# Short convolution's input projection as seven products of halves, with both modulation streams started later

## The chip, the cores and the metric

The kernel runs on one core of a Trainium2 chip. The metric is the device time of one execution in microseconds (us); of several runs the median is taken. TensorE is called PE, VectorE DVE, GpSimd POOL. SyncE (SP) only issues transfers from device memory here.

## The reference

The program is a network in float32 on 512 tokens of width 1024: first four layers with attention mixers, then a second block of two layers. The second block's layer 0 is a hybrid mixer and a feed-forward network; its layer 1 is the short convolution and a feed-forward network. What the change touches is this:

```python
mod = silu(c) @ ada_w[i] + ada_b[i]                  # 1024 -> 6 x 1024, for layer i
sh1, sc1, g1, sh2, sc2, g2 = split(mod, 6)

def shortconv_mixer(h, w_in, conv_w, w_out):         # w_in: 1024 x 3072
    gb, gc, u = split(h @ w_in, 3, axis=-1)
    return (gb * dw_conv(gc * u, conv_w)) @ w_out    # 3 taps over the tokens

x = x + g1 * shortconv_mixer(modulate(rms_norm(x, norm_mix[i]), sh1, sc1), ...)
x = x + g2 * swiglu(modulate(rms_norm(x, norm_ffn[i]), sh2, sc2), ...)
```

## The kernel before

Everything is kept with features on the 128 partitions and tokens along them, so `x` and the normed, modulated `h` are eight tiles of 128x512. Each engine has its own program, and semaphores order them.

**Weights.** SP loads slots of up to 1 MB (1024 input features by 256 output features) into the two halves of `ring`. The load of slot i+1 waits until PE has begun with slot i (`slot_begun`, given by the first matmul on a slot). For the short convolution SP loads twelve slots, for each of four groups g of 256 features the gate gc, then u, then gb.

**The short convolution before.** `short_convolution` on PE runs `pair_of_tiles` for each slot (L1680): two tiles of eight matmuls 128x512 each (L727), in banks 0 and 1 in turn. ScalarE copies the two gate tiles to `sc_gate`; DVE multiplies the tiles of u by them into the padded `sc_pad` (L3161), runs `convolve` (three operations over 512 tokens, all in SBUF, L2856 to L2858) into `sc_sum`, and multiplies the tiles of gb by it into `og` (L3169). `out_projection_of_parts` (L921) then multiplies `og` by the output weights; its first eight products need og's tiles 0 to 3, the next ones wait for tiles 4 to 7 one by one.

**Seven products, in the feed-forward networks.** `ffn` computes a product of a slot (both dimensions halved: a11, a12, a21, a22) and `h` (input features and tokens halved: b11, b12, b21, b22) in seven products of halves instead of eight. A slot is a chunk: seven parts of four matmuls 128x256 (`part`, L1588), in the order p1 = a11 b11, p2 = a12 b21, p6, p5, p7, p3, p4; `first_parts` runs the first two, `other_parts` the other five. The five need sums: four of weights, which DVE makes for each chunk from the slot (`sum_weights`, four operations 128x512, L3024 to L3031, told by `weights_summed`), and four differences of `h` made once (`sum_moving`, L3044, told by `moving_summed`). A chunk has three PSUM banks (`BANK_SETS`), and p6 is accumulated on what p1 left in its bank, and so on; so ScalarE copies three states of banks (`snaps`, L2225, told by `snap_read`), and DVE adds them to the final states: after p2 (L3070), after p7 (L3075) and after p3 (L3077); the fourth quarter is ready after p4. PE waits for the addition after p7 before it runs p4 in the same bank, and for a chunk's weight sums before `other_parts`. In `gated_pair` of the network, DVE's weight sums for the next chunk stand between the addition after p2 and the one after p7. The first two chunks run their first parts one behind the other, while the differences and sums are made.

**Modulation.** POOL computes `mod` in nine jobs (`job`), each a stream of 24 steps of 512 KB: a transfer into one of two buffers (L657), a multiplication by a column of silu(c) (TENSOR_SCALAR, L669), and an addition to `ada_sum` (TENSOR_TENSOR, L673), both with all operands in SBUF. A job begins when the last one's sums are read (`mods_ready`). Job 7 (`ada_w_2[1]`, first half) therefore begins at the start of the first network (`ffn(7)` on PE), and is wanted at its end; job 8 (second half) begins at the start of the short convolution and is wanted at the end of its output projection. Both are wanted in `result_squares`, which sums squares of the result for the norm on PE and turns the modulation sums into columns (L782). Behind it the norm runs: root on ScalarE, reciprocal on DVE (L2406), spread on PE, `normed` on DVE (L2416) and `shift` on ScalarE (L1784), tile by tile, each told by `h_ready`.

## Time and profile before

| | us |
|---|---|
| median of 3 runs | 2848.08 |
| lowest, highest | 2843.29, 2850.89 |
| the profiled execution | 2844.35 |
| its span, first to last instruction | 2842.5 |
| PE busy | 2699.3 (95%) |
| DVE busy | 1314.0 (46%) |
| POOL busy | 1069.4 (38%) |
| ScalarE busy | 659.5 (23%) |

| stretch of the span | from, to (us) |
|---|---|
| first network, its first two chunks | 1753.15 to 1789.90 |
| first network, all | 1753.15 to 2177 |
| short convolution, products of the input projection | 2184.54 to 2349.42 |
| its output projection | 2349.42 to 2404.44 |
| last network, its first two chunks | 2412.33 to 2442.93 |

In the profile, lengths are in us, times are counted from the first instruction, and what stands in brackets behind an instruction is how long its engine idled before it and what released it. A matmul of float32 shows as two records. The mean granted clock of TensorE is 0.980 of full speed.

### The profile page before, as it was taken

The page shows a single profiled execution, that of the slowest core. Times are in us where ns is not written, and L with a number is a line of the kernel's source. Part 1 is how long each engine was busy: PE and PEld are TensorE (multiplying, and loading weights), DVE is VectorE, ACT ScalarE, POOL GpSimd, SP SyncE. Part 2 cuts the span into 40 slices and gives each one's busy share as a digit, 9 for nine tenths or more (in the row PEclk, how much of TensorE's full clock was granted, in tenths as well). Part 3 has the DMA queues.
Part 4 walks back from the last instruction along what each step waited for, and adds up shares of the span by engine and source line. Part 5 has one row for each costly group of instructions (what it writes and reads, how often), then busy time and mean ns, then how long its engine had stood idle before and what let it go on. Part 6 is the DMA issues. An engine that isn't in the chain of part 4 may idle for free.

```text
span 2842.5 us, 32196 instructions
## 1 busy us (share of the span) xinstructions
PE 2699.3 (95%) x11791; PEld 1768.6 (62%) x11791; DVE 1314.0 (46%) x2667; ACT 659.5 (23%) x1575; POOL 1069.4 (38%) x574
## 2 busy tenths in 40 slices
PE   6799999998999999899998899899999999999997
PEld 5356544465666544465645565788887444888886
DVE  7133367334556643333555663443554322433554
ACT  2133123322333432232214522111101001111101
POOL 4785188048583005850683002870001880000000
PEclk7899999999999999999999999999999999999999
DMA  7342343145342114332441003452223542222222
GB/s 244 106 129 92 95 131 115 59 117 147 83 126 53 30 45 124 115 94 59 120 140 38 1 16 99 147 153 89 85 82 99 164 148 74 74 89 85 83 88 71
DMA packets 245112, 277.81 MB, mean 98 GB/s; under 512 B 41427, under 2 KB 217824, under 8 KB 244864
## 3 DMA queue, kind: packets, MB, share of 16 engines
q1 hardware_dynamic: 216000, 175.03, 20.3%
q0 software_dynamic: 28224, 100.86, 11.5%
q8 instruction: 78, 1.28, 0.2%
q14 instruction: 42, 0.34, 0.0%
q10 hardware_dynamic: 768, 0.30, 0.0%
HBM read 274.06 MB, written 2.10 MB: 97 GB/s over the span
## 4 chain that ended last, share of the span: by engine, by line
PE 86%; DVE 4%; DMA 3%; ACT 2%; issue 2%; POOL 1%; SPq 1%; DVEq 0%; ACTq 0%; POOLq 0%
PE psum L1588 27%; PE psum L727 20%; PE psum L921 12%; PE psum L1101 7%; PE psum L895 3%; PE psum L1267 2%; PE psum L782 2%; PE psum L1285 1%; PE psum L907 1%; PE psum L1060 1%; PE psum L1061 1%; PE psum L1419 1%; PE psum L1123 1%; DMA ring<-in_ffn_w_gate 1%; POOL ada_ring L669 1%
## 5 line engine op out<-in xcount | busy, mean ns | idle before, releaser
L657 POOL DMA_DIRECT2D ada_ring<-in_ada_w x192 | 114.8, 598 | 1251.9 <-DVEq L2401 803.6
L727 PE MATMUL psum<-h,ring 128*128 128x512 f32 (+1 forms) x1280 | 538.9, 580 | 16.2 <-DVE arena L2345 4.7
L669 POOL TENSOR_SCALAR ada_ring<-ada_ring,cond 128x1024 f32<-128x1024 f32 x168 | 479.7, 2856 | 8.4 <-POOL ada_sum L673 2.1
L727 PEld LDWEIGHTS psum<-h,ring 128*128 128x128 f32 x1280 | 243.1, 192 | 295.4 <-issue 277.0
L673 POOL TENSOR_TENSOR ada_sum<-ada_sum,ada_ring 128x1024 f32<-128x1024 f32 x168 | 396.9, 2363 | 14.9
L921 PE MATMUL psum<-og,ring 128*128 128x512 f32 x768 | 334.9, 595 | 0.3
L1588 PE MATMUL psum<-og,arena 128*128 128x256 f32 x1152 | 258.6, 379 | 1.7 <-ACT probs L2225 1.7
L921 PEld LDWEIGHTS psum<-og,ring 128*128 128x128 f32 x768 | 145.2, 191 | 180.1 <-issue 180.1
L1588 PEld LDWEIGHTS psum<-og,arena 128*128 128x128 f32 x1152 | 218.7, 190 | 32.1 <-issue 2.4
L1101 PE MATMUL psum<-h,ring 128*128 128x512 f32 x496 | 229.4, 593 | 1.4 <-DVE arena L2473 1.4
L1819 ACT ACTIVATE probsT<-psum 128x128 f32<-128x128 f32 (+3 forms) x232 | 104.5, 451 | 338.9 <-PE psum L895 338.4
L1588 PE MATMUL psum<-h,ring 128*128 128x256 f32 x768 | 178.5, 383 | 1.6 <-DVE mods L2399 0.9
L1588 PEld LDWEIGHTS psum<-h,ring 128*128 128x128 f32 x768 | 146.2, 192 | 26.2 <-ACT h L1784 5.1
L2499 DVE CUSTOM_DVE_ANT_0 psum<-psum,cst 128x128 f32<-128x128 f32 (+1 forms) x192 | 95.3, 498 | 121.3 <-PE psum L1267 83.2
L1101 PEld LDWEIGHTS psum<-h,ring 128*128 128x128 f32 x496 | 87.8, 191 | 81.8 <-issue 81.0
L1852 ACT ACTIVATE sq<-x 128x512 f32<-128x512 f32 x63 | 39.8, 631 | 424.7 <-DVE x L2565 228.4
L2225 ACT ACTIVATE probs<-psum 128x256 f32<-128x256 f32 x132 | 50.8, 385 | 373.5 <-PE psum L1588 373.5
L3101 DVE SCALAR_TENSOR_TENSOR x<-psum,mods,x 128x256 f32<-128x256 f32 x168 | 81.2, 483 | 112.1 <-PE psum L1588 110.8
L2565 DVE SCALAR_TENSOR_TENSOR x<-psum,mods,x 128x512 f32<-128x512 f32 x48 | 36.0, 751 | 204.3 <-PE psum L921 203.8
L1808 ACT ACTIVATE psum<-psum,neg_max 128x256 f32<-128x256 f32 (+3 forms) x256 | 122.7, 479 | 23.7 <-DVE neg_max L2499 22.1
L895 PE MATMUL psum<-cst,arena 128*128 128x128 f32 x608 | 110.9, 284 | 10.6 <-ACT probsT L1819 7.0
L1769 ACT ACTIVATE arena<-psum 128x512 f32<-128x512 f32 (+4 forms) x100 | 55.1, 558 | 281.9 <-PE psum L727 228.8
(387 smaller groups left out, 3818.0 us busy)
## 6 DMA issues: line engine op xcount, KB each, us to landing
ada_ring<-in_ada_w POOLq DMA_DIRECT2D x192, 512.0 KB, 4.1
ring<-in_ffn_w_gate SPq DMA_DIRECT2D x22, 1024.0 KB, 5.3
ring<-in_ffn_w_up SPq DMA_DIRECT2D x22, 1024.0 KB, 5.4
ring<-in_ffn_w_down SPq DMA_DIRECT2D x16, 1024.0 KB, 5.2
ring<-in_sc_w_in SPq DMA_DIRECT2D x12, 1024.0 KB, 5.8
ring<-in_mla_w_in SPq DMA_DIRECT2D x10, 1024.0 KB, 5.5
ring<-in_mla_w_out SPq DMA_DIRECT2D x8, 1024.0 KB, 5.1
ring<-in_swa_w_in SPq DMA_DIRECT2D x16, 512.0 KB, 5.5
```

Source lines behind the costliest of these rows:

```text
L657: pool.dma_start(ada_ring[:, i % 2, :], w[k * P:(k + 1) * P, first(part)]).then_inc(arrived[i % 2], n.give(f"ada_in{i % 2}", 16))
L669: step = nc.gpsimd.tensor_scalar(piece, ada_ring[:, i % 2, :], c, None, ALU.mult)
L673: step = nc.gpsimd.tensor_tensor(total, total, piece, ALU.add)
L727: m = pe.matmul(tile.at[:, part], lhs(k), rhs(k), start=(k == 0), stop=(k == K - 1))
L895: m = pe.transpose(bank[:, i * P:(i + 1) * P], p[:, block_at:block_at + P], ident)
L921: m = pe.matmul(out_tiles[c].at, w8(out_slots[0], P * (c % 2))(k), og[:, k * T:(k + 1) * T], start=(k == 0), stop=(k == KT - 1))
L1101: m = pe.matmul(made["tile"].at, weights(made)(k), h_lat(k), start=(k == 0), stop=(k == KT - 1))
L1588: last = pe.matmul(out, weights[:, k, :], moving[:, k, :], start=begins and k == 0, stop=True, skip_group_check=True)
L1808: e = nc.scalar.activation(scored, scored, ACT.Exp, bias=neg_max[:, step % 4, g:g + 1], scale=scale, accum_out=row_sum[:, step % 4, g:g + 1])
L1819: c = nc.scalar.activation(probsT[:, i % 2, 0:w], PB[:, 0:w], ACT.Copy)
L2499: last = nc.vector.tensor_tensor_reduce(s[:, at:at + w], s[:, at:at + w], mask(u), -scale, floor, ALU.add, ALU.min, neg_max[:, b, g:g + 1])
L3101: nc.vector.scalar_tensor_tensor(xq, bank, scales[q], xq, ALU.mult, ALU.add).then_inc(S[told], n.give(told))
```

## The change

- PE: `short_convolution` runs twelve chunks of seven parts with the functions of the networks, in place of 24 tiles. At its end it waits for all readings of the chunks before the last.
- DVE: the differences of `h` go to a new place in the arena (`sc_moving`). In each chunk the order is: addition after p2; (in chunks of gb) the convolution of the first tile, in the last chunk that of the second too; additions after p7 and after p3; (in chunks of gb) the multiplication of the first tile into `og`; the weight sums of the next chunk; the other products or the second convolution; what needs p4. The weight sums of the first chunk are made at the end of the network before (`first_weights_of("sc")`).
- ScalarE: three copies of bank states per chunk, in place of the copies of gate tiles.
- PE, `result_squares` of the first network: it lets SP load the second slot of the short convolution.
- POOL: job 7 begins when the first network has finished three turns of its first loop (`hid_ready` 3, six chunks), job 8 when the short convolution has finished its first two chunks (`part_done` 252). The loop over jobs 5 and 6 stays a loop; 7 and 8 are written out.

The diff, with its added lines (those that it removes stand in the code above):

```diff
@@ -479,6 +479,8 @@
+        sc_moving = [view(4096 + 1024 * i, 4, HALF) for i in range(4)]
+        SC_CHUNKS = 12
@@ -683,11 +685,16 @@
             sums_read()
             job(A["ada_w_2"][0], lambda part: slice(part * CHUNK, (part + 1) * CHUNK), 16, range(2))
...
+            with turns(pool, 2, n, per) as half:
+                sums_read()
+                job(A["ada_w_2"][0], lambda part: ds(half * JOB_W + part * CHUNK, CHUNK), 8)
+            for half in range(2):
+                sums_read()
+                if half == 0:
+                    pool.wait_ge(S["hid_ready"], 3)
+                else:
+                    pool.wait_ge(S["part_done"], 7 * (FT + 3 * KT // 2) + 14)
+                job(A["ada_w_2"][1], lambda part, half=half: slice(half * JOB_W + part * CHUNK, half * JOB_W + (part + 1) * CHUNK), 8)
@@ -1675,11 +1682,37 @@
                 n.take("moving_summed", 12)
...
+                result_squares(job, frees_slot=job is not None)
             def short_convolution():
...
+                snap0, sum0 = n.of["snap_read"].at, n.of["sum_read"].at
+                MARK["ffn", "sc"] = (slots[0], n.of["slot_full0"].at, n.of["slot_full1"].at)
+                h0 = n.take("h_ready", KT) - KT
+                moving = halves_of(h[:, :, 0:T], 4)
+                t0 = n.of["moving_summed"].at
+                n.take("moving_summed", 4)
+                def chunk(c):
+                    return Chunk(open_slot(), 4, c % 2, moving, sc_moving, lambda k: snap0 + 3 * c + k,
+                                 lambda k: sum0 + 4 * c + k)
+                first, second = chunk(0), chunk(1)
+                for bank in (0, 1):
+                    evacuated_last(bank)
+                first_parts(first, slot_begins=False, fresh=h0)
+                first_parts(second, slot_begins=False)
+                other_parts(first, moving_ready=t0 + 3)
+                other_parts(second, slot_begins=True)
+                for c in range(2, SC_CHUNKS):
+                    pe.wait_ge(S["snap_read"], snap0 + 3 * (c - 1))
+                    pe.wait_ge(S["sum_read"], sum0 + 4 * (c - 1))
+                    following = chunk(c)
+                    first_parts(following)
+                    other_parts(following)
+                pe.wait_ge(S["snap_read"], snap0 + 3 * (SC_CHUNKS - 1))
+                pe.wait_ge(S["sum_read"], sum0 + 4 * (SC_CHUNKS - 1))
+                n.take("snap_read", 3 * SC_CHUNKS)
+                n.take("sum_read", 4 * SC_CHUNKS)
@@ -2245,11 +2278,15 @@
             def short_convolution():
...
+                begun = n.of["part_done"].at
+                for c in range(SC_CHUNKS):
+                    p1, p2, p6, p5, p7, p3, p4 = FIRST_PARTS_DONE[c] if c < 2 else [7 * c + k for k in PARTS_DONE[0]]
+                    r1, r2, r3 = [psum[:, b, early] for b in BANK_SETS[c % 2]]
+                    for snap, (part, bank) in enumerate(((p1, r1), (p6, r1), (p5, r2))):
+                        act.wait_ge(S["part_done"], begun + part)
+                        nc.scalar.activation(snaps[c % 2][snap], bank, ACT.Copy).then_inc(S["snap_read"], n.give("snap_read"))
+                n.take("part_done", 7 * SC_CHUNKS)
+                n.take("sum_read", 4 * SC_CHUNKS)
@@ -3146,30 +3183,71 @@
                 add_square(KT - 2)
+                if job == 6:
+                    first_weights_of("sc")
             def short_convolution():
...
+                h_at = n.of["h_scaled"].at
+                halves = halves_of(h[:, :, 0:T], 4)
+                for which, k in ((1, 4), (3, 8), (2, 8), (4, 8)):
+                    dve.wait_ge(S["h_ready"], h_at - KT + k)
+                    sum_moving(halves, sc_moving, which)
+                sum_weights(1, 4)
+                begun, snapped = n.of["part_done"].at, n.of["snap_read"].at
+                for c in range(SC_CHUNKS):
+                    g, kind = c // 3, c % 3
+                    p1, p2, p6, p5, p7, p3, p4 = FIRST_PARTS_DONE[c] if c < 2 else [7 * c + k for k in PARTS_DONE[0]]
+                    r1, r2, r3 = [psum[:, b, early] for b in BANK_SETS[c % 2]]
+                    snap = snaps[c % 2]
+                    put = [[sc_gate[:, q, :] for q in range(2)], [sc_pad[:, q, 1:1 + T] for q in range(2)],
+                           [og[:, (2 * g + q) * T:(2 * g + q + 1) * T] for q in range(2)]][kind]
+                    factor = [None, sc_gate, sc_sum][kind]
+                    def convolved(i, g=g):
+                        taps = [cols[:, group, row + 8 * tap + 2 * g + i:row + 8 * tap + 2 * g + i + 1] for tap in range(3)]
+                        return convolve(sc_sum[:, i, :], sc_pad[:, i, :], T, taps)
+                    dve.wait_ge(S["part_done"], begun + p2)
+                    dve.wait_ge(S["snap_read"], snapped + 3 * c + 1)
+                    nc.vector.tensor_tensor(put[0][:, early], r3, snap[0], ALU.add).then_inc(S["sum_read"], n.give("sum_read"))
+                    if kind == 2:
+                        settle(convolved(0))
+                        if c == SC_CHUNKS - 1:
+                            settle(convolved(1))
+                    dve.wait_ge(S["part_done"], begun + p7)
+                    dve.wait_ge(S["snap_read"], snapped + 3 * c + 3)
+                    nc.vector.tensor_tensor(put[1][:, late], r1, snap[2], ALU.add).then_inc(S["sum_read"], n.give("sum_read"))
+                    dve.wait_ge(S["part_done"], begun + p3)
+                    nc.vector.tensor_tensor(put[0][:, late], r2, snap[1], ALU.add).then_inc(S["sum_read"], n.give("sum_read"))
+                    dve.wait_ge(S["sum_read"], n.now("sum_read"))
+                    if kind == 2:
+                        nc.vector.tensor_tensor(put[0], put[0], factor[:, 0, :], ALU.mult
+                                                ).then_inc(S["og_ready"], n.give("og_ready"))
+                    if 0 < c < SC_CHUNKS - 1:
+                        sum_weights((c + 1) % 2, 4)
+                    if kind == 1:
+                        settle(nc.vector.tensor_tensor(put[0], put[0], factor[:, 0, :], ALU.mult))
+                    elif kind == 2 and c < SC_CHUNKS - 1:
+                        settle(convolved(1))
+                    dve.wait_ge(S["part_done"], begun + p4)
+                    if kind == 0:
+                        nc.vector.tensor_copy(put[1][:, early], r1).then_inc(S["sum_read"], n.give("sum_read"))
+                        dve.wait_ge(S["sum_read"], n.now("sum_read"))
+                        continue
+                    nc.vector.tensor_tensor(put[1][:, early], r1, factor[:, 1, early], ALU.mult
+                                            ).then_inc(S["sum_read"], n.give("sum_read"))
+                    last = nc.vector.tensor_tensor(put[1][:, late], put[1][:, late], factor[:, 1, late], ALU.mult)
+                    if kind == 2:
+                        dve.wait_ge(S["sum_read"], n.now("sum_read"))
+                        last.then_inc(S["og_ready"], n.give("og_ready"))
+                        continue
+                    settle(last)
+                    dve.wait_ge(S["sum_read"], n.now("sum_read"))
+                n.take("part_done", 7 * SC_CHUNKS)
+                n.take("snap_read", 3 * SC_CHUNKS)
```

## Rows read from the trace of the kernel before

**Rows 1.** The page's first part, busy time, share of the span and instructions by engine:
```profile
PE 2699.3 (95%) x11791; PEld 1768.6 (62%) x11791; DVE 1314.0 (46%) x2667; ACT 659.5 (23%) x1575; POOL 1069.4 (38%) x574
```

**Rows 2.** The chain that ended last: start, length (us), what; short convolution:
```profile
2184.57 165.01 PE psum L727 x384
```

**Rows 3.** Stages: us, PE, PEld, DVE, ACT, POOL busy (instructions), PEclk, DMA, GB/s:
```profile
1753.15:1789.90 36.75, 27.90 (x113) 21.93 (x114) 21.24 (x25) 8.85 (x17) 27.87 (x15) 0.89 0.37 115
1789.90:1909.81 119.91, 111.98 (x505) 95.85 (x504) 57.65 (x77) 16.84 (x41) 103.83 (x53) 0.99 0.51 158
1817.18:1831.74 14.56, 12.36 (x58) 10.56 (x57) 7.05 (x10) 2.12 (x5) 12.82 (x7) 1.00 0.51 162
2184.54:2349.42 164.88, 164.88 (x386) 73.04 (x386) 41.03 (x50) 9.41 (x16) 132.34 (x69) 1.00 0.48 153
2412.33:2442.93 30.60, 27.31 (x112) 21.47 (x113) 16.44 (x25) 8.85 (x17) 0.00 (x0) 0.96 0.11 35
2442.93:2692.00 249.07, 249.07 (x1153) 219.21 (x1152) 102.08 (x182) 38.94 (x92) 0.00 (x0) 1.00 0.28 89
```

**Rows 4.** Timeline, PE, last network: start, length, instructions; first parts of two chunks:
```profile
2455.55 3.62 PE L1588 MATMUL psum<-h,ring 128*128 128x256 f32 x16
...
2467.64 3.62 PE L1588 MATMUL psum<-h,ring 128*128 128x256 f32 x16
```

**Rows 5.** Timeline, PE, longest wait at both networks' starts, in brackets the releaser:
```profile
1786.32 3.78 PE L1588 MATMUL psum<-og,ring 128*128 128x256 f32 x8 [7.66 <-DVE arena L3075]
...
2439.95 3.19 PE L1588 MATMUL psum<-og,ring 128*128 128x256 f32 x8 [2.10 <-DVE arena L3075]
2442.93 4.15 PE L1588 MATMUL psum<-h,ring 128*128 128x256 f32 x16
```

**Rows 6.** Timeline, DVE, last network, POOL idle: differences of h, weight sums, addition:
```profile
2416.18 2.35 DVE L3044 TENSOR_TENSOR og<-h 128x1024 f32<-128x1024 f32 x2
...
2461.75 0.69 DVE L3024 TENSOR_TENSOR arena<-ring 128x512 f32<-128x512 f32 x1 [1.89 <-DMA ring<-in_ffn_w_gate]
...
2463.68 0.69 DVE L3031 TENSOR_TENSOR arena<-ring,arena 128x512 f32<-128x512 f32 x1
...
2466.23 0.42 DVE L3077 TENSOR_TENSOR arena<-psum,probs 128x256 f32 x1 [1.18 <-PE psum L1588]
```

**Rows 7.** Timeline, POOL, first network, job 7's stream:
```profile
1797.52 2.85 POOL L669 TENSOR_SCALAR ada_ring<-ada_ring,cond 128x1024 f32<-128x1024 f32 x1
...
1878.10 2.34 POOL L673 TENSOR_TENSOR ada_sum<-ada_sum,ada_ring 128x1024 f32<-128x1024 f32 x1
```

**Rows 8.** Timeline, DVE, weight sums in the same stretch:
```profile
1798.15 1.04 DVE L3024 TENSOR_TENSOR arena<-ring 128x512 f32<-128x512 f32 x1 [3.00 <-DMA ring<-in_ffn_w_up]
...
1878.24 2.75 DVE L3031 TENSOR_TENSOR arena<-ring,arena 128x512 f32<-128x512 f32 x1
```

**Rows 9.** Groups by line, from 2000 us on: busy, mean ns; the convolution's steps:
```profile
L2856 DVE TENSOR_SCALAR arena<-arena,cols 128x512 f32<-128x512 f32 x8 | 5.9, 733 | 1.2 <-DVE arena L3161 0.5
...
L2857 DVE SCALAR_TENSOR_TENSOR arena<-arena,cols 128x512 f32<-128x512 f32 x8 | 10.2, 1274 | 1.2 <-DVE arena L2856 0.2
...
L2858 DVE SCALAR_TENSOR_TENSOR arena<-arena,cols 128x512 f32<-128x512 f32 x8 | 10.5, 1316 | 1.2 <-DVE arena L2857 0.2
```

**Rows 10.** Timeline, DVE, a convolution's second step, not blocked:
```profile
2330.68 0.75 DVE L2857 SCALAR_TENSOR_TENSOR arena<-arena,cols 128x512 f32<-128x512 f32 x1
```

**Rows 11.** Timeline, DVE and ScalarE, start of the short convolution:
```profile
2180.38 0.95 DVE L2406 RECIPROCAL rms<-rms 128x128 f32<-128x128 f32 x1 [3.38 <-ACT rms L1873]
...
2185.84 2.73 DVE L2416 SCALAR_TENSOR_TENSOR h<-x,gains,psum 128x512 f32<-128x512 f32 x4 [0.15 <-DVE mods L2399]
...
2186.63 2.70 ACT L1784 ACTIVATE h<-h,mods 128x512 f32<-128x512 f32 x4 [0.25 <-DVE h L2416]
```

**Rows 12.** Timeline, POOL, first and last instruction of job 8's stream:
```profile
2186.47 0.60 POOL L657 DMA_DIRECT2D ada_ring<-in_ada_w  x1 [273.74 <-DVEq L2401]
...
2344.51 2.34 POOL L673 TENSOR_TENSOR ada_sum<-ada_sum,ada_ring 128x1024 f32<-128x1024 f32 x1
```

More of the change, by code:

```diff
@@ L684, in _ @@
             job(A["ada_w_2"][0], lambda part: slice(part * CHUNK, (part + 1) * CHUNK), 16, range(2))
-            with turns(pool, 2, n, {k: 2 * v for k, v in per.items()}) as t:
-                with turns(pool, 2, n, per) as half:
-                    sums_read()
-                    job(A["ada_w_2"][ds(t, 1)].rearrange("l k n -> (l k) n"),
-                        lambda part: ds(half * JOB_W + part * CHUNK, CHUNK), 8)
+            with turns(pool, 2, n, per) as half:
[8 more added lines that the diff above has]
+                job(A["ada_w_2"][1], lambda part, half=half: slice(half * JOB_W + part * CHUNK, half * JOB_W + (part + 1) * CHUNK), 8)
         @block.tensor
@@ L1677, in ffn @@
                 pe.wait_ge(S["sum_read"], n.of["sum_read"].at - 4)
-                result_squares(job)
+                result_squares(job, frees_slot=job is not None)
             def short_convolution():
-                for i in range(12):
-                    pair_of_tiles(fresh=(i == 0))
+                snap0, sum0 = n.of["snap_read"].at, n.of["sum_read"].at
[24 more added lines that the diff above has]
+                n.take("sum_read", 4 * SC_CHUNKS)
             def block2_tensor():
@@ L2247, in short_convolution @@
             def short_convolution():
-                with turns(act, 2, n, {"tile": 12}):
-                    for g in range(2):
-                        for i in range(2):
-                            copy_tile((sc_gate[:, i, :], whole))
-                        skip(4)
+                begun = n.of["part_done"].at
[7 more added lines that the diff above has]
+                n.take("sum_read", 4 * SC_CHUNKS)
             def block2_scalar():
```

18 lines of the change are left out of this document (removed).

## The prediction

> **What bounds the kernel now.** The page's first part shows TensorE (PE) busy for 95% of the span [rows 1]; the other engines matter only where PE waits for them. The chain of work that ended last, over the short convolution, shows one unbroken piece of PE [rows 2]: neither VectorE (DVE), ScalarE nor the weight DMAs hold the stage. The table by stages [rows 3] gives 164.88 us for its 192 products of 128x512. The feed-forward networks show what seven products of halves cost: without GpSimd (POOL) activity a chunk starts every 12.09 us (2467.64 less 2455.55) [rows 4]. That is 28 matmuls of 128x256 at 0.432 us; a matmul has two records, and a part of four takes 1.73 us. The reader should then look at how such a stage stalls: at its first weight sums [rows 5], and while POOL works on a modulation stream [rows 3, 7, 8].
>
> The sum is made against the profiled execution: 2844.35 us, 1.85 above its span. The median of the three timed runs lies 3.73 above it, and I carry that distance over.
>
> **1. The products.** 12 slots of 16 matmuls of 128x512 become 12 chunks of 28 of 128x256: 12 x 12.09 = 145.1 us against 164.88. **-19.8 us** on PE, all on the chain. The number of weight loads rises by 3/4, but the 249.07 us of the last network's busy stretch holds 1153 records at 0.216 us each [rows 3], so the loads stay behind the matmuls.
>
> **2. The start of the stage.** Before, a product of 0.86 us outlasts the making of an h tile (four in 2.7 us [rows 11]), so PE never waited. Now the eighth tile is ready at 2186.63 + 2.70 = 2189.3; behind it stand one matmul and eight of the second chunk: 2193.3, against 2184.54 + 6.9 = 2191.4 without waits. **+1.9 us.** Differences of h: DVE is through with h at 2188.6, and three differences of 1.2 us [rows 6] end at 2192.2; the one-column memsets ahead of them have 1.1 us to spare under 2193.3. The second chunk's weight sums end at 2196.5 and are wanted 8.6 us after 2193.3. Upper bound: the last network's start, 30.60 us for two chunks worth 24.18 [rows 3], +6.4. I stay near the low end, because the largest wait in it (2.10 us [rows 5]) is DVE waiting for the third slot's weights with an addition queued behind; here those sums come behind the additions. The first chunk's weight sums (2.6 us) are moved to DVE's idle time ahead of the reciprocal, 3.38 us [rows 11]: nothing, with 0.7 us to spare, and 1:1 on the chain beyond that. The second slot's load starts at the sums of squares, some 7 us earlier: nothing.
>
> **3. DVE in a steady chunk.** Per chunk DVE now has three additions of 0.42, four weight sums (2461.75 to 2464.37: 2.62) [rows 6] and one or two products; in every third chunk also two convolutions. ScalarE's three copies stay beside it. Two waits can take PE's place. (a) The addition of the fifth part must end about 10.3 us after the chunk's start, when PE wants the bank again. (b) The next chunk's weight sums must end by 12.09 + 3.45 = 15.5. With POOL idle the addition of the sixth part starts at 10.68 (2466.23 less 2455.55), ends at 11.1, and behind a 0.15 us wait the sums run to 13.9: 1.6 us of slack. In a chunk that ends in og, a product of 0.68 stands ahead: slack 0.95. So without POOL nothing stalls.
>
> POOL isn't idle: job 8's stream, 160.4 us long [rows 12], now lies over chunks 2 to 11. A DVE operation with both inputs in SBUF waits for POOL's TENSOR_TENSOR: started 0.14 us behind one of 2.34 us, a weight sum took 2.75 instead of 0.69; behind the 2.85 us TENSOR_SCALAR (started 0.63 before it) another took 1.04 [rows 7, 8], so that one blocks for about its first us. Of the eleven sets of four sums under job 7's stream, six were longer by 2.0 to 2.2 us (2.75 is one of them), one by 3.4, one by 0.7, the rest by under 0.4. Over (b)'s slack that leaves on average 0.4 us for the six chunks (3, 4, 6, 7, 9, 10) with 1.6, and 1.0 for the three (2, 5, 8) with 0.95, whose product can be blocked too: 2.4 + 3.0. For (a): a chunk with og finds DVE free 5.4 us in on average (in the chunk before it the sums end at 13.9 + 1.4 on average, and three products of 0.68, 0.42 and 0.42 with gaps and blocks, 2.2, follow: 17.5 less 12.1); then 0.42, one convolution at its stretched means of 0.73 + 1.27 + 1.32 with three gaps of 0.15 [rows 9] (3.8), and the addition 0.42 end at 10.1, close under 10.3. I take 0.5 us for each of three, and 0.2 for each of the three chunks after them, where the second convolution has run late: 2.1. Sum **+7.5 us**, about 0.8 a chunk. Bounds: nothing (all slack holds), and the longest cycle of the first network, 14.56 us [rows 3], at nine chunks: 9 x 2.47 = 22.2. I stay below that network's own mean under the stream (119.91 / 9 = 13.32, so 1.2 a chunk), because there each additional 2 us on the sums stood directly ahead of the addition that PE waited for.
>
> What the rule would make of it: the Trainium skill, SBUF — State Buffer, section "SBUF: two separate sides", has the port shared by the two engines as an exclusive lock, held for the whole instruction. By it POOL's multiplication too would block for its 2.85 us; the 1.04 us row speaks against that. If it held, a set would meet 1.9 us more, and (b) would cost up to 17 us more.
>
> **4. The last chunk.** Both convolutions stand ahead of its fifth part's addition: free at 5.4, then 0.42 + 2 x 3.8 + 0.42 = 13.8, wanted at 10.3: **+3.5 us**. Bounds: 0.5 with the unblocked durations (0.75 [rows 10] for two of a convolution's three steps), 6 with two long blocks more. The output projection's first eight products (6.9 us) then cover the last two multiplications into og.
>
> **5. The streams.** Job 7's stream started with the first network's first products: 36.75 us for two chunks against 30.60 [rows 3], with a 7.66 us wait [rows 5], 6.15 too much; the nine cycles after it took 119.91 instead of 108.8, of which 0.5 is clock: 10.6. In all 16.7 us. It now starts after three turns, near 1833, ends near 1993 (wanted at 2177), and meets steady chunks only: 160.4 / 13.3 = 12.1 chunks at 1.15 (10.6 over nine is 1.18) = 13.9. **-2.8 us.** Bounds: 0.9 to 1.6 a chunk, so -5.8 to +2.7. Job 8's stream now starts 26 us into the short convolution and ends near 2371; its sums are wanted at about 2184.5 + 158 + 55 = 2397. Nothing, with 26 us in hand. POOL's queue holds nothing else.
>
> **Sum.** -19.8 + 1.9 + 7.5 + 3.5 - 2.8 = -9.7 us: 2834.7 in the profiled execution's terms, **2838.4 us** against the median. A clock at its lower level after a long stall is in the bounds: PE idled 2.10 us, and the next eight records took 2.98 us (2442.93 less 2439.95) instead of 1.73 [rows 5].
>
> **Rivals.**
> A. *The slack holds.* POOL and PE fall into step so that the blocks miss the weight sums, as in four of the eleven sets. Steady stalls 1 us, last chunk 1 us, streams -5.8: -19.8 + 1.9 + 1 + 1 - 5.8 = -21.7, **2826.4 us**. For it: those four lost under 0.8 us. Against: POOL blocks 2.34 and about 1 us of each of its 24 steps of 160.4 / 24 = 6.7 us, half of the time.
> B. *The gain goes into the steady wait.* Stalls at the first network's pace, 9 x 1.2 = 11; last chunk 6; streams 0: -19.8 + 1.9 + 11 + 6 = -0.9, **2847 us**. For it: that pace was measured with the same sums and the same POOL work. Against: the additions now stand ahead.
> C. *DVE becomes the bound of the stage.* Convolutions, products and sums blocked at nearly every POOL instruction, so that each chunk under the stream takes 14.56 us; it decides from 1.6 us of stall a chunk (19.8 - 1.9 over eleven chunks), with the streams at zero. -19.8 + 1.9 + 22.2 + 6 = +10.3, **2858 us**. For it: a convolution's third step took 1.32 us on average against 0.75 unblocked [rows 9, 10]. Against: in three chunks DVE has nine additions, twelve sums, two convolutions and eight products or copies, 20 us unblocked and, by the stretched durations, some 30, in 36.3 of PE's.
> D. *The change doesn't remove PE time*, the weight loads becoming the bound: excluded nearly by the 1153 records in 249.07 us; below 2 in 100.
>
> **How the numbers follow.** Forecast 0.56, A 0.20, B 0.16, C 0.06, D 0.02. A measurement of this kernel tells 0.3% (8.5 us) from no change. The forecast's own range is -16 to -3 us (2832 to 2845); some 6 in 10 of it lie beyond -8.5, which gives faster 0.34 + 0.20 = 0.54, same 0.22 + 0.16 = 0.38, slower 0.08 (C and D). The range takes in A and B: 2825 to 2850.
>
> **What would show it.** Chunks of the short convolution start every 12.1 us on the timeline while POOL is idle (chunks 0, 1), the first at about the old time. PE's waits in the stage name DVE: the weight sums' last step for (b), the addition behind it for (a), the latter longest in the last chunk, 1 to 6 us. Under POOL's stream the cycle averages 12.9 us; 12.2 would be A, 13.3 B, 14.5 C. The first network's first two chunks take 30.6 us, and 11 to 12 later ones 13.2. I would be wrong on the whole if PE waited for ScalarE's copies or for slot loads in the short convolution, if the output projection waited for og, or if the sums of squares after it waited for job 8.

## The result and the profile after

The median is 2832.19 us (2825.68 to 2851.14) against 2850.89 us for the kernel before (2838.28 to 2855.18) on the same chips. The ratio is 0.9948, with a 95% interval of 0.9938 to 0.9959: **-14.8 us** (-11.7 to -17.7). The two medians alone lie 18.7 us apart; the figure used here is the ratio. The forecast was -9.7 us.

The profiled execution took 2835.45 us with a span of 2833.8, 8.7 less than before. Half of that is no effect of the change: the first network's first product started at 1748.82 instead of 1753.15 [rows 3], and nothing ahead of it was changed (over the kernels below it varied from 1744.2 to 1753.6). A profile is also a single execution: the one before ran 6.5 us below the median of its kernel (2844.35 against 2850.89), the one after 3.3 above (2835.45 against 2832.19). So the profiles are read by stages here, and totals are taken from the timed runs.

The page's first part after (to be held against [rows 1]; PE has 288 instructions more and is busy 23 us less):
```profile
PE 2676.5 (94%) x12079; PEld 1819.9 (64%) x12079; DVE 1392.2 (49%) x2767; ACT 665.6 (23%) x1603; POOL 1073.3 (38%) x574
```

Stages of the changed kernel, with the columns of [rows 3]: the first network from its first product to the sums of squares, and from these to the output projection's first product. The latter took 172.27 us before, 7.39 ahead of the 164.88 of [rows 3].
```profile
1748.82:2174.15 425.33, 408.51 (x1848) 352.93 (x1849) 213.54 (x344) 52.24 (x117) 135.92 (x69) 0.99 0.34 109
2174.15:2342.08 167.93, 155.85 (x744) 135.09 (x745) 122.52 (x154) 19.43 (x46) 117.60 (x62) 0.97 0.47 144
```

The short convolution gained 4.3 us here, and the first network, 424.00 before, lost 1.3. PE's timeline shows what the second stage consists of: the start, the third chunk's start, the longest wait in a steady chunk, the last chunk and the first output product.
```profile
2182.95 7.59 PE L1595 MATMUL psum<-h,ring 128*128 128x256 f32 x32 [1.38 <-ACT h L1817]
...
2207.64 3.62 PE L1595 MATMUL psum<-h,ring 128*128 128x256 f32 x16
...
2260.49 5.45 PE L1595 MATMUL psum<-arena 128*128 128x256 f32 x24 [0.42 <-DVE arena L3068]
...
2317.81 3.62 PE L1595 MATMUL psum<-h,ring 128*128 128x256 f32 x16
...
2326.44 1.89 PE L1595 MATMUL psum<-h,arena 128*128 128x256 f32 x8
2338.51 3.78 PE L1595 MATMUL psum<-arena,ring 128*128 128x256 f32 x8 [10.18 <-DVE og L3222]
2342.08 55.32 PE L928 MATMUL psum<-og,ring 128*128 128x512 f32 x128
```

Chunks 2 to 10 took 110.17 us, 1.4 over nine times 12.09. The last took 24.27, **12.2 over**: a wait of 10.18 for the fifth part's addition (L3222), then eight records in 3.57 us instead of 1.73. DVE's timeline shows what the addition stood behind, the six steps of the two convolutions (L2893 to L2895):
```profile
2325.57 1.35 DVE L2893 TENSOR_SCALAR arena<-arena,cols 128x512 f32<-128x512 f32 x1
2326.95 2.71 DVE L2894 SCALAR_TENSOR_TENSOR arena<-arena,cols 128x512 f32<-128x512 f32 x1
2329.70 2.03 DVE L2895 SCALAR_TENSOR_TENSOR arena<-arena,cols 128x512 f32<-128x512 f32 x1
2331.76 1.43 DVE L2893 TENSOR_SCALAR arena<-arena,cols 128x512 f32<-128x512 f32 x1
2333.23 2.70 DVE L2894 SCALAR_TENSOR_TENSOR arena<-arena,cols 128x512 f32<-128x512 f32 x1
2335.96 2.03 DVE L2895 SCALAR_TENSOR_TENSOR arena<-arena,cols 128x512 f32<-128x512 f32 x1
2338.03 0.42 DVE L3222 TENSOR_TENSOR og<-psum,probs 128x256 f32<-128x256 f32 x1
```

The same stretch on POOL, job 8's stream:
```profile
2326.72 2.39 POOL L675 TENSOR_TENSOR ada_sum<-ada_sum,ada_ring 128x1024 f32<-128x1024 f32 x1
2329.41 0.60 POOL L659 DMA_DIRECT2D ada_ring<-in_ada_w  x1 [0.30 <-POOL ada_sum L675]
2330.06 2.85 POOL L671 TENSOR_SCALAR ada_ring<-ada_ring,cond 128x1024 f32<-128x1024 f32 x1
2333.00 2.38 POOL L675 TENSOR_TENSOR ada_sum<-ada_sum,ada_ring 128x1024 f32<-128x1024 f32 x1
```

From addition to addition these steps are 6.28 us; in the kernel before they were 160.4 / 24 = 6.7 [rows 12]. POOL issues the next transfer 0.30 us after an addition. Each second step of a convolution began 0.23 us behind an addition of POOL and ended 0.55 us after it; each third step began just ahead of a multiplication, 0.36 us ahead in both convolutions.

### The profile page after: what moved, and what is told of

Its sections match the earlier page's. It is cut to its first block, busy times and chain, and to the rows that moved or that the text cites. A ratio compares the mean times of both kernels' runs of the same rounds, so it can differ in the third digit from the quotient of the medians.

```text
span 2833.8 us, 32664 instructions
## 1 busy us (share of the span) xinstructions
PE 2676.5 (94%) x12079; PEld 1819.9 (64%) x12079; DVE 1392.2 (49%) x2767; ACT 665.6 (23%) x1603; POOL 1073.3 (38%) x574
## 4 chain that ended last, share of the span: by engine, by line
PE 84%; DVE 5%; DMA 4%; issue 2%; ACT 2%; POOL 1%; SPq 1%; DVEq 0%; ACTq 0%; POOLq 0%
PE psum L1595 30%; PE psum L734 14%; PE psum L928 12%; PE psum L1108 7%; PE psum L902 3%; PE psum L1274 2%; PE psum L789 2%; PE psum L1292 1%; PE psum L914 1%; PE psum L1067 1%; PE psum L1068 1%; DMA ring<-in_ffn_w_up 1%; DMA ring<-in_ffn_w_gate 1%; PE psum L1426 1%; PE psum L1130 1%
## 5 line engine op out<-in xcount | busy, mean ns | idle before, releaser
L734 PE MATMUL psum<-h,ring 128*128 128x512 f32 (+1 forms) x896 | 371.7, 572 | 15.3 <-ACT arena L1802 3.7
L734 PEld LDWEIGHTS psum<-h,ring 128*128 128x128 f32 x896 | 169.3, 192 | 201.9 <-issue 184.4
L1595 PE MATMUL psum<-h,ring 128*128 128x256 f32 x960 | 221.1, 381 | 3.0 <-ACT h L1817 2.1
L1595 PEld LDWEIGHTS psum<-h,ring 128*128 128x128 f32 x960 | 181.5, 190 | 33.0 <-ACT h L1817 5.8
L1595 PE MATMUL psum<-arena 128*128 128x256 f32 x640 | 148.2, 379 | 0.4 <-DVE arena L3068 0.4
L1108 PEld LDWEIGHTS psum<-h,ring 128*128 128x128 f32 x496 | 88.4, 192 | 82.9 <-issue 82.1
L1595 PE MATMUL psum<-h,arena 128*128 128x256 f32 x576 | 136.1, 379 | 0.0
L1595 PEld LDWEIGHTS psum<-arena 128*128 128x128 f32 x640 | 121.4, 190 | 17.8 <-DVE arena L3068 1.4
```

What stands on the lines that cost most here:

```text
L734: m = pe.matmul(tile.at[:, part], lhs(k), rhs(k), start=(k == 0), stop=(k == K - 1))
L1108: m = pe.matmul(made["tile"].at, weights(made)(k), h_lat(k), start=(k == 0), stop=(k == KT - 1))
L1595: last = pe.matmul(out, weights[:, k, :], moving[:, k, :], start=begins and k == 0, stop=True, skip_group_check=True)
```

## The experiments

Each ratio is to the kernel before, with its 95% interval; "the stage" is the stretch from the sums of squares to the first output product.

**The streams without the convolution.** In the kernel before, POOL's loop over jobs 5 to 8 becomes a loop over jobs 5 and 6, with jobs 7 and 8 written out behind it (job 8 starts at its old place):
```diff
-            with turns(pool, 2, n, {k: 2 * v for k, v in per.items()}) as t:
-                with turns(pool, 2, n, per) as half:
...
+            with turns(pool, 2, n, per) as half:
...
+            for half in range(2):
+                sums_read()
+                if half == 0:
+                    pool.wait_ge(S["hid_ready"], 3)
...
```


> The kernel before with POOL's part of the change alone: jobs 7 and 8 written out, job 7 begins after three turns of the first network, job 8 at the old place. Theory 1 (the gain is the short convolution's products, the streams bring almost nothing): the first network's start takes 33 instead of 36.8 us, but the steady chunks under the stream give 3 to 5 us back; first network 424 to 426 us, total 0 to 3 us under before (ratio 0.999 to 1.000). Rival (half of the gain of the change is the streams, 10 us and more): ratio 0.997 or below.

Measured: 0.9995 (0.9981 to 1.001). The first network took 420.0 us in its profile, the stage 172.3; that execution ran 7.4 us below its kernel's median (2835.76 against 2843.18). The forecast's own term, -2.8 us, is within the interval (-5.4 to +2.8), and so is no effect at all.

**The convolution without the streams.** The changed kernel with POOL's old loop and starts (the edit above, reversed).

> The changed kernel with POOL's old part: both jobs in the loop and at their old starts, so job 8's stream lies over chunks 0 to 11 of the short convolution. Theory 1: nearly the whole gain stays, 10 to 14 us under before (ratio 0.995 to 0.9965); the first chunks lose 1 to 4 us more than in the changed kernel, the last chunk still waits 5 to 12 us for the addition behind both convolutions. Rival (the streams carry the gain): 0 to 6 us under before.

Measured: 0.9992 (0.9981 to 1.0004). The stage took 170.1 us: 2.7 over at its start, 5.7 over in the steady chunks, 9.2 in the last. PE's waits in steady chunks are now for weight sums, four of them (0.56 to 1.29 us), and the last chunk has one of 1.25 ahead of its wait for the addition. Three of the four, and that last wait:
```profile
2266.96 5.45 PE L1590 MATMUL psum<-arena 128*128 128x256 f32 x24 [1.28 <-DVE arena L3063]
...
2293.52 5.45 PE L1590 MATMUL psum<-arena 128*128 128x256 f32 x24 [1.29 <-DVE arena L3063]
...
2319.45 5.45 PE L1590 MATMUL psum<-arena 128*128 128x256 f32 x24 [1.24 <-DVE arena L3063]
...
2345.93 3.78 PE L1590 MATMUL psum<-arena,ring 128*128 128x256 f32 x8 [5.70 <-DVE og L3217]
```
Either half alone is no measurable change, and the two together are 0.9948. So the parts' gains don't add up.

**The last chunk's order.** In the changed kernel the last chunk's second convolution goes behind the additions, as in the other chunks:
```diff
                         settle(convolved(0))
-                        if c == SC_CHUNKS - 1:
-                            settle(convolved(1))
...
-                    elif kind == 2 and c < SC_CHUNKS - 1:
+                    elif kind == 2:
```


> The changed kernel, but in the last chunk too the second convolution comes behind the additions that TensorE waits for. Theory 1 (the 12 us in the last chunk are DVE's two convolutions, blocked by POOL, ahead of that addition): the wait in the last chunk falls from 10.2 us to 1 to 4, no time at the lower clock behind it, og's last tiles are ready under the output projection's first products or 1 to 2 us late: 6 to 10 us under the changed kernel, ratio to before 0.991 to 0.993. Rival (DVE's work only moves, the output projection then waits as long for og): within 2 us of the changed kernel, with the wait at the output projection's seventh and eighth products of the first tile.

Measured: 0.9943 (0.9927 to 0.9959), not to be told from the change. The last chunk was 6.0 over instead of 12.2: the first convolution alone, at 1.35, 2.71 and 2.03 us a step, still made PE wait 3.98.

**POOL's arithmetic taken away.** Job 8 multiplies and adds 8 columns of each piece instead of 1024 (its transfers stay; the rest of the second network's modulation sums is left out):
```diff
-                            nc.gpsimd.tensor_scalar(piece, ada_ring[:, i % 2, :], c, None, ALU.mult)
+                            nc.gpsimd.tensor_scalar(piece, ada_ring[:, i % 2, 0:width], c, None, ALU.mult)
...
```


> The changed kernel with job 8's multiplications and additions on 8 columns instead of 1024 (its transfers stay; the last network's modulation is then not computed from all columns). Theory 1 (every wait of a chunk beyond the start is DVE blocked by POOL's operations): the short convolution takes 147 to 149 us from first to last product, 12.09 a chunk, with at most 1 us of wait in the last chunk; 11 us under the changed kernel, ratio 0.990 to 0.992. Rival (both convolutions in the last chunk are too long by themselves): a wait of 3 us or more is left in the last chunk.

Measured: 0.9906 (0.9889 to 0.9923). The stage's row:
```profile
2169.99:2324.34 154.35, 152.97 (x744) 134.26 (x745) 84.45 (x154) 19.46 (x46) 30.61 (x64) 1.00 0.50 159
```
Every chunk took 12.09 us, the last too. From the first product to the output projection's it is 145.55 us, with DMA as busy as before. So transfers, slot loads, ScalarE's copies and the weight loads cost nothing, and all of the 13.6 us over in the steady and last chunks of the changed kernel's profile comes from POOL's arithmetic. DVE is busy 84.45 us instead of 122.52 with the same 154 instructions.

**The changed kernel once more**, unedited.

> The changed kernel once more, beside the others of this call. The stage of the short convolution should repeat the first profile (its chunks are paced by semaphores and job 8 starts from one of them): 1.4 us of steady waits, 10 us and the lower clock in the last chunk, 168 us from the sums of squares to the output projection. If the last chunk's wait differs by over 2 us, it depends on how POOL happens to lie. The first network: 417 to 425 us.

Measured: 0.9933 (0.9914 to 0.9951). The profiled execution was the fastest of its six (2819.33 us, median 2826.41). Its stages:
```profile
1745.91:2164.05 418.14, 403.72 (x1849) 349.48 (x1850) 217.42 (x344) 52.29 (x117) 135.57 (x69) 1.00 0.35 111
2164.05:2325.75 161.70, 155.62 (x744) 134.85 (x745) 116.60 (x154) 19.42 (x46) 111.64 (x58) 0.99 0.48 147
```
The steady chunks are as before (1.4 over), but the last was 6.0 over, with this wait and these six steps on DVE:
```profile
2322.39 3.57 PE L1595 MATMUL psum<-arena,ring 128*128 128x256 f32 x8 [4.18 <-DVE og L3222]
```
```profile
2313.70 1.69 DVE L2893 TENSOR_SCALAR arena<-arena,cols 128x512 f32<-128x512 f32 x1
2315.43 0.75 DVE L2894 SCALAR_TENSOR_TENSOR arena<-arena,cols 128x512 f32<-128x512 f32 x1
2316.22 0.75 DVE L2895 SCALAR_TENSOR_TENSOR arena<-arena,cols 128x512 f32<-128x512 f32 x1
2317.01 2.54 DVE L2893 TENSOR_SCALAR arena<-arena,cols 128x512 f32<-128x512 f32 x1
2319.58 0.75 DVE L2894 SCALAR_TENSOR_TENSOR arena<-arena,cols 128x512 f32<-128x512 f32 x1
2320.37 1.51 DVE L2895 SCALAR_TENSOR_TENSOR arena<-arena,cols 128x512 f32<-128x512 f32 x1
```
They took 7.99 us and the other execution's 12.25; DVE also reached the chunk's first addition 5.67 us into the chunk instead of 7.42. The same code has two patterns, by where POOL's instructions happen to lie: here the one multiplication began at 2313.99, and two steps ran free behind its first 1.4 us. One profile doesn't size this term.

**The written-out streams as loops of one turn**, to get the old step of POOL at the new starts.

> The changed kernel, with jobs 7 and 8 at their new starts but each in a loop of one turn, their addresses worked out from the turn as before. Theory 2 (the written-out streams have a shorter step, 6.3 instead of 6.7 us, because the transfer is issued after 0.30 us instead of 0.65 to 0.76, and that step sets TensorE's pace under the stream): POOL's gap is again 0.65 to 0.76 us, the first network's chunks under the stream take 13.3 instead of 12.97 us, the short convolution's steady waits rise from 1.4 to 5 to 7 us: 6 to 10 us over the changed kernel, ratio to before 0.997 to 0.999. Rival (only the starts matter): within 2 us of the changed kernel.

Measured: 0.9958 (0.9942 to 0.9974). POOL still issued 0.30 us behind its additions, so the step wasn't lengthened, and this says nothing of the step. It is a further execution of the same pattern: 168.6 us for the stage, 12.3 over in the last chunk.

**The same in one loop of two turns**, whose addresses and wait depend on the turn:
```diff
+            with turns(pool, 2, n, per) as half:
+                sums_read()
+                pool.wait_ge(S["hid_ready"], 3)
+                pool.wait_ge(S["part_done"], half * (7 * (FT + 3 * KT // 2) + 13) + 1)
+                job(A["ada_w_2"][1], lambda part: ds(half * JOB_W + part * CHUNK, CHUNK), 8)
```


> The changed kernel with jobs 7 and 8 at their new starts in one loop of two turns (a loop of one turn had left POOL's gap at 0.30 us, so it tested nothing of the step). Theory 2 (POOL's step, not only the starts, carries the gain): gap 0.65 to 0.76 us and a step of 6.65 us; steady waits in the short convolution of 4 to 7 us in all as in e2b_conv (0.5 to 1.3 us at the weight sums of most chunks) instead of 1.4; ratio to before 0.997 to 0.999. Rival (only the starts matter): 1 to 2 us of steady waits, ratio 0.993 to 0.996.

Measured: 0.9948 (0.9929 to 0.9967). Here the step was long, by the issue behind the addition (POOL), and the steady chunks waited for weight sums (PE):
```profile
2237.84 2.85 POOL L671 TENSOR_SCALAR ada_ring<-ada_ring,cond 128x1024 f32<-128x1024 f32 x1
2240.78 2.34 POOL L675 TENSOR_TENSOR ada_sum<-ada_sum,ada_ring 128x1024 f32<-128x1024 f32 x1
2243.83 0.61 POOL L659 DMA_DIRECT2D ada_ring<-in_ada_w  x1 [0.72 <-POOL ada_sum L675]
2244.48 2.85 POOL L671 TENSOR_SCALAR ada_ring<-ada_ring,cond 128x1024 f32<-128x1024 f32 x1
```
```profile
2239.56 5.45 PE L1593 MATMUL psum<-arena 128*128 128x256 f32 x24 [1.24 <-DVE arena L3066]
```

The steady chunks were 8.5 over, with five such waits (1.23 to 1.34), and the last 3.4 over, with 2.12 of wait: 166.3 us for the stage. Two sums of the set that this wait is for were stretched (0.69 us each when free), the first by a whole addition of POOL:
```profile
2234.25 2.85 DVE L3061 TENSOR_TENSOR arena<-ring 128x512 f32<-128x512 f32 x1
...
2237.73 1.78 DVE L3066 TENSOR_TENSOR arena<-ring,arena 128x512 f32<-128x512 f32 x1
```

So the longer step costs 7 us more in the steady chunks. The last chunk's waits were shorter in this profile, but not with the same step in the convolution without the streams (9.2 over), and no total changed that can be measured.

**The old order of the weight sums.** In the changed kernel the short convolution's weight sums go ahead of the fifth part's addition, where the networks have them:
```diff
+                    if 0 < c < SC_CHUNKS - 1:
+                        sum_weights((c + 1) % 2, 4)
                     dve.wait_ge(S["part_done"], begun + p7)
...
-                    if 0 < c < SC_CHUNKS - 1:
-                        sum_weights((c + 1) % 2, 4)
                     if kind == 1:
```


> The changed kernel with the short convolution's weight sums ahead of the addition of the fifth part, as in the networks. Theory 1 (the order is what keeps the steady waits at 1.4 us): the steady chunks of the short convolution wait 1 to 2.5 us each for the addition, 10 to 20 us in the stage more, ratio to before 0.999 to 1.003. Rival (the order does not matter, POOL's block does): within 3 us of the changed kernel.

Measured: 1.0025 (1.0007 to 1.0043), slower than the kernel before. The stage took 190.9 us: 3.9 over at its start, 26.5 in the steady chunks, 8.0 in the last. Eight of the nine steady chunks show a wait for an addition (0.47 to 5.15 us), the ninth one of 0.2; the longest is one where a convolution and the sums stand ahead of it. The stage's row and that wait:
```profile
2177.35:2368.24 190.89, 164.90 (x744) 139.75 (x745) 127.76 (x154) 19.46 (x46) 135.46 (x69) 0.94 0.43 133
```
```profile
2271.71 3.78 PE L1595 MATMUL psum<-arena,ring 128*128 128x256 f32 x8 [5.15 <-DVE og L3224]
```

**The same order in the networks.** Three kernels put their weight sums behind the additions too (the names are those of the changed kernel):
```diff
-                    if i or not first:
-                        sum_weights(1 - i, 4)
                     dve.wait_ge(S["part_done"], at.now(p7))
...
                     nc.vector.tensor_tensor(put[0][:, late], r2, snaps[i][1], ALU.add)
+                    if i or not first:
+                        sum_weights(1 - i, 4)
```
In the kernel before, that alone:

> The kernel before with one edit: in both networks the weight sums of the next chunk come behind the additions that TensorE waits for. Theory 3 (DVE's order decides what POOL's stream costs a chunk): the first network falls from 424 to 427 us to 405 to 410 although job 7's stream lies over its start, the last network's start to 28 to 29 us; ratio to before 0.993 to 0.9945. Rival (the gain of 12 us in e6_ffn needs the late, short-stepped stream): first network 415 us or more, ratio 0.997 or above.

Measured: 0.9924 (0.9904 to 0.9944). By its middle value that is more than the whole change under study (0.9948), though the intervals overlap. The first network took 417.8 us and waited eight times for weight sums (2.37 once, then 1.30 to 1.42) while POOL worked:
```profile
1747.12:2164.91 417.79, 403.40 (x1848) 349.55 (x1849) 219.72 (x343) 52.73 (x117) 135.91 (x69) 1.00 0.34 111
```
Its length is the rival's, the ratio is the theory's and better. The last network's first two chunks took 27.1 us instead of 30.6. The 6.2 and 3.5 us of these two stretches are about half of the 22 us that the ratio stands for; the profile before, 6.5 us below its kernel's median, understates them.

In the changed kernel, that alone:

> The changed kernel with the networks' weight sums behind the additions, both convolutions of the last chunk left ahead of its addition (e6_ffn without the edit of e3b_last). If the last chunk's order matters: its wait is 4 or 10 us against none in e6_ffn, ratio to before 0.988 to 0.992 against 0.987. If it doesn't (the wait depends only on how POOL lies): under 2 us between them.

Measured: 0.9885 (0.9865 to 0.9905). The first network took 405.1 us, the stage 168.5 with the same 10.18 us wait in its last chunk.

In the changed kernel with the last chunk's order of above:

> As the kernel with the last chunk's second convolution behind the additions (e3b_last), and in both networks too the weight sums of the next chunk behind the additions that TensorE waits for. Expected: the wait at the networks' starts (2 to 4 us, with the lower clock behind it) goes, and the chunks of the first network under the stream take 12.1 to 12.5 us instead of 12.97: first network 405 to 411 us instead of 417, last network's start 27.5 instead of 29.4 to 30.6. Ratio to before 0.988 to 0.991. Rival (the sums are then late for the next chunk's third part): waits of the same length at the weight sums, no gain over e3b_last's 0.9943.

Measured: **0.9871** (0.9852 to 0.989), 2807.78 us. Its stages:
```profile
1745.71:2150.77 405.06, 402.01 (x1849) 349.97 (x1849) 218.24 (x344) 52.74 (x117) 134.36 (x69) 1.00 0.36 114
2150.77:2308.86 158.09, 154.56 (x744) 133.71 (x745) 116.02 (x152) 19.47 (x46) 106.22 (x56) 1.00 0.47 147
```
It beats both kernels, by 37 us the one before. That the last chunk's order adds to it was seen in the stage (158.1 against 168.5 us) and is not settled in time: the two intervals overlap.

The same with POOL's old loop and starts:

> e6_ffn (all weight sums and the last chunk's second convolution behind the additions) with POOL's old part: loops, old starts, step 6.65 us. Theory 3: with this order the starts matter less; first network 406 to 411 us, short convolution 161 to 168 us (steady waits at the weight sums remain); ratio to before 0.989 to 0.992. Rival (starts and step matter as much as before): 0.4% over e6_ffn, 0.991 or above, with the loss in the first network.

Measured: 0.9873 (0.9854 to 0.9892). The first network took 410.3 us, the stage 163.1. With the weight sums behind the additions everywhere, the place and the step of the streams were worth nothing that can be measured.

## Why the prediction held and where it missed

The direction and the range were right; the forecast was 5 us short, and it came that near partly by luck, since two terms were wrong in opposite directions. By its own steps:

**1. Products: right.** -19.8 us. Without POOL's arithmetic the twelve chunks took 145.55 us, and 0.5 of it belongs to the start. Rival D is out.

**2. The start: right.** +1.9 us: 8.80 us to the first product (7.39 before) and 24.69 for two chunks worth 24.18. Most of it shows as a wait of 1.38 ahead of the first product. The profile puts that down to h, but the first product needs only the first tile of h, made by 2181.4; the program also has PE wait there until both product banks are read (`evacuated_last`), and DVE's reading of the modulation sums (L2436) ended at 2182.70, 0.25 us ahead of PE's start. In the first network PE began 0.26 us behind the same instruction, and there the profile names it. It cost nothing in the end: the eighth tile of h came at 2186.34 (before, the same 12.2 us behind the sums of squares), PE's weight load waited for it, and the nine matmuls from there on end the first parts, as forecast:
```profile
2182.54 0.16 DVE L2436 TENSOR_TENSOR mods<-psum,cols 128x8 f32<-128x8 f32 x1
...
2186.39 3.75 PEld L1595 LDWEIGHTS psum<-h,ring 128*128 128x128 f32 x18 [0.36 <-ACT h L1817]
```

**3. The steady chunks: mis-sized, +7.5 against a measured 1.4.** The kind of wait was right: where POOL's step was the old one, the same waits for weight sums cost 5.7 and 8.5 us. The step that failed is what POOL's blocks leave "over (b)'s slack", 0.4 us a chunk for six chunks and 1.0 for three. It was taken from job 7's sets under looped code with steps of some 6.7 us, where six of eleven met an addition of POOL and were longer by 2.0 to 2.2 us. Written out, job 8 took 151 us (2208.40 to 2359.66), and its steps fell elsewhere: all nine sets under it were hit, but by 0.8 to 1.8 us, mostly within the slack that was worked out (1.6 and 0.95). In the loop of two turns six of nine sets met a whole addition again (one sum of 2.83 to 2.85) and were 2.2 to 3.3 us longer. The 2.1 us for (a) shrank too, to a gap of 0.27. With the short step the term was 1.4 to 1.9 in five profiles and 3.7 in the best kernel's. The longest set of the changed kernel, with two blocks of 0.9 us each, ended at 2247.28, in time by 0.1:
```profile
2242.84 1.58 DVE L3061 TENSOR_TENSOR arena<-ring 128x512 f32<-128x512 f32 x1
2244.34 0.70 DVE L3063 TENSOR_TENSOR arena<-ring 128x512 f32<-128x512 f32 x1
2244.96 1.60 DVE L3066 TENSOR_TENSOR arena<-arena,ring 128x512 f32<-128x512 f32 x1
2246.59 0.69 DVE L3068 TENSOR_TENSOR arena<-ring,arena 128x512 f32<-128x512 f32 x1
```
Rival A had the right size for this term (1 us), but not the reason: the blocks didn't miss the sums, they were short. That the order is what keeps it low is shown by the old order's 26.5 us, even above the bound of 22.2 that rival C used. Rival C's reason doesn't hold there either, since DVE was busy 127.76 of 190.89 us; what PE waited for is the order of DVE's work. What was said against rival B, that the additions now stand ahead, decided this term.

**4. The last chunk: mis-sized, +3.5 with a bound of 6 against a measured 12.2 or 6.0.** The convolution was priced at its mean of 3.8 us [rows 9]. That mean comes from stretches in which a block hits some steps. In the first profile six steps follow each other without a pause, and each second step meets the next addition of POOL: 6.1 to 6.2 us a convolution. Two such are 12.3, where 7.6 was put. The other 2 us are DVE's late arrival (7.42 instead of 5.4), blocked as well. The clock added 1.85: after the long stall the granted clock was 0.50, the lower level, where it had been 1.00:
```profile
2328.00:2332.00 4.00, 0.33 (x2) 0.00 (x0) 3.93 (x3) 0.00 (x0) 3.66 (x3) 1.00 0.26 63
2332.00:2336.00 4.00, 0.00 (x0) 0.00 (x0) 3.93 (x3) 0.00 (x0) 3.61 (x3) 0.54 0.17 68
...
2340.00:2342.00 2.00, 2.00 (x6) 1.64 (x5) 0.00 (x0) 0.00 (x0) 1.71 (x1) 0.50 0.00 0
```
In the other execution the mean was about right: the two convolutions took 8.0 us and PE's wait was 4.18, near the 3.5. There the clock is what the term left out: it went down behind this shorter wait too, and the eight records took 3.36 us (2325.75 less 2322.39) instead of 1.73. The forecast had the clock in its bounds only. Its lower bound of 0.5 doesn't follow from its own figures (5.4 + 0.42 + 2 x 2.68 + 0.42 = 11.6, which is 1.3 over 10.3); nothing hangs on it.

The errors of 3 and 4 have opposite signs: together 11 were forecast and 13.6 or 7.4 measured.

**5. The streams: -2.8, not told from nothing.** Alone they gave -1.4 us with an interval on both sides of zero. The first network took 424.0 and 427.2 us with the old starts (the kernel before, and the convolution alone), and 425.3, 420.0, 417.0, 416.5, 418.1, 425.7, 423.4 and (with the short convolution's sums in the old order) 430.0 with the new ones, 422.0 on average: about -4, within the bounds, with a scatter as large as the term. Two details missed. Its first two chunks took 32.96 us, not 30.6, with a wait of 4.40 for an addition behind the sums of a slot whose transfer was issued at 1768.09 and landed 7.6 us later, before job 7's stream began; in the other execution it landed in 6.2, and they took 30.31. And the steady cycle under the stream wasn't 13.2 throughout: mostly 12.97, which is two of POOL's steps (6.22 and 6.75), with two long ones of 16.3 and 17.0 in the changed kernel's profile. Job 8's stream ended at 2359.7, some 38 us before PE wanted its sums.

**The sum.** The stage's terms, with the measured sizes, give -19.8 + 1.9 + 1.4 + 12.2 = -4.3 or, in the other pattern, -10.5; its profiles say -4.3 and -10.6. With -4 for the first network that is -8 to -14; the measured -14.8 (-11.7 to -17.7) lies at its far end. Two things not in that count point the same way: from the output projection on the two profiles of the changed kernel were 1.1 and 1.4 us shorter than the one before (492.0 and 491.7 against 493.1), and the profile before is of a fast execution. The forecast of -9.7 thus rested on two mis-sized terms that partly cancel, and the profiles account for most of what was measured, not surely for all.

**What stays open.** Parts 1 to 4 alone gave -2.3 us (interval -5.4 to +1.1) where this count of the forecast was -6.9, the streams alone -1.4, both -14.8. The profiles show less of that: first network and stage together took 596.3 us before, 597.3 with the convolution alone, 592.3 with the streams alone, and 593.3 and 579.8 with both. POOL's shorter step doesn't look like the joint part: with the long step at the new starts the ratio was again 0.9948. The new starts are left, but they gave nothing alone, and nothing once the networks had the other order. Their worth therefore depends on how waits lie in the first network, and these runs don't say more.

**The rule that was weighed.** Under POOL's addition a second step of 0.75 us took 2.71; behind the first 1.4 us of a multiplication the same step took 0.75 (2315.43). A first step, 0.48 us when free, did not end before the multiplication did when it began 1.8 us into it (2325.57). The Trainium skill, SBUF — State Buffer, section "SBUF: two separate sides", calls the shared port an exclusive lock for a whole instruction: the first row agrees, the second doesn't, and the third would fit it. Nor was it enough to begin first: the third step at 2329.70 began 0.36 us ahead of a multiplication and took 2.03 us, and the multiplication its usual 2.85.

## What to carry to other kernels

Where PE waits for one result of an engine, put that result ahead of everything that has slack, in every stage that has the pattern: this order was worth some 22 to 26 us here in the short convolution (1.0025 against 0.9948 and 0.9933) and some 20 more in the networks (0.9924 against 1, 0.9885 against 0.9948). Price a chain of instructions without pauses by its blocked durations too, and not by their mean alone: the same six steps took 7.99 us in one execution and 12.25 in another. Add the lower clock where a wait of that kind is forecast for PE: here it stood behind waits of 2.10 [rows 5], 2.12, 4.18 and 10.18 us. And read a stage's gain from its own stretch in more than one execution: two of the same kernel differed by 16 us of span.

## What the hardware showed beyond that

- POOL's written-out transfers were mostly issued 0.30 us behind the addition ahead of them, those with an address from a loop's turn 0.64 to 0.84. That made steps of 6.2 to 6.3 us instead of 6.6 to 6.7 where DVE didn't hold POOL up. Loops of one turn behaved as written-out code.
- DVE and POOL hold up each other. In the first network POOL's addition at 1865.39 took 2.87 us instead of 2.34; a weight sum of DVE had begun at 1865.36.
- Engines that wait for each other's work can fall into step. A network's chunk settled at 12.97 us, two of POOL's steps (6.22 and 6.75, the longer with such a stretched addition), and PE waited 0.60 to 0.73 us in chunk after chunk. With the long step it settled at 13.76 (6.65 and 7.11).
- PE at rest for some 10 us came back at a granted clock of 0.50, and eight records took 3.57 us instead of 1.73. After 4.18 us at rest they took 3.36, and after 2.12 (the loop of two turns) 2.85.
